# Two 64-column stationary tiles in place of one of 128, in the level products of a delta scan

## What is computed

```python
kk = jnp.einsum('bhntd,bhnsd->bhnts', k, k)
M = jnp.eye(CHUNK, dtype=jnp.float32) + jnp.where(strict, kk * decay * beta[..., :, None], 0.0)
...
U = lax.linalg.triangular_solve(M, v * beta[..., None], left_side=True, lower=True, unit_diagonal=True)
Wk = lax.linalg.triangular_solve(M, k * (beta * eG)[..., None], left_side=True, lower=True, unit_diagonal=True)
```

## Time and profile before

| | us |
|---|---|
| median of 3 runs | 3254.94 |
| lowest and highest run | 3253.11, 3256.28 |
| span of the profiled execution | 3254.3 |
| PE busy in that span | 3039.7 (93%) |
| weight loads busy (PEld) | 2229.6 (69%) |
| DVE busy | 963.2 (30%) |
| ACT busy | 577.3 (18%) |
| stretch of the delta scan in that span | 1946 to 2352 |

### The profile page before, as it was taken

One profiled execution on the slowest core, in us unless ns is written; L12 is line 12 of the kernel. 1 busy time (PEld: TensorE's weight loads), 2 busy tenths in 40 slices (PEclk: granted clock), 3 DMA queues, 4 the chain that ended last, 5 costly groups with the idle time before them and its releaser, 6 DMA issues.

```text
span 3254.3 us, 43264 instructions
## 1 busy us (share of the span) xinstructions
PE 3039.7 (93%) x18405; PEld 2229.6 (69%) x18405; DVE 963.2 (30%) x2408; ACT 577.3 (18%) x1297; POOL 96.0 (3%) x145
## 2 busy tenths in 40 slices
PE   6999999797999999997999989999986999999994
PEld 1465479745887777771456459999944888777773
DVE  1100136643001000102177536666645010001002
ACT  3100111240000000003167212222242000000002
POOL 0000000000000000000000000000000000000000
PEclk9899998897999999998999999999997999999997
DMA  8411100217999999957411100000016899999992
GB/s 281 154 52 52 45 1 1 65 62 270 312 311 303 303 309 308 306 183 271 155 52 52 39 0 1 1 2 1 1 65 224 279 314 304 307 305 307 306 310 87
DMA packets 276365, 545.50 MB, mean 168 GB/s; under 512 B 15233, under 2 KB 23817, under 8 KB 276233
## 3 DMA queue, kind: packets, MB, share of 16 engines
q1 hardware_dynamic: 175049, 328.64, 29.4%
q10 hardware_dynamic: 93600, 188.75, 16.6%
q0 software_dynamic: 7584, 26.22, 3.2%
HBM read 517.89 MB, written 25.70 MB: 167 GB/s over the span
## 4 chain that ended last, share of the span: by engine, by line
PE 88%; DVE 6%; ACT 3%; DMA 2%; issue 1%; SPq 0%; DVEq 0%; POOL 0%; ACTq 0%
PE ps L1204 28%; PE ps L1215 14%; PE ps L803 8%; PE ps L813 6%; PE ps L760 5%; PE ps L1139 3%; PE ps L1101 3%; PE ps L804 2%; PE ps L1083 2%; PE ps L880 1%; PE ps L1115 1%; PE ps L791 1%; PE ps L950 1%; PE ps L966 1%; ACT L424 1%; ACT L423 1%
## 5 line engine op out<-in xcount | busy, mean ns | idle before, releaser
L1204 PEld LDWEIGHTS ps<-wk,slots 128*128 128x128 f32 x6144 | 691.1, 192 | 16.5 <-issue 16.0
L1204 PE MATMUL ps<-wk,slots 128*128 128x80 f32 x6144 | 689.9, 275 | 0.0
L1215 PE MATMUL ps<-qkv,og 128*80 128x512 f32 x1024 | 446.7, 594 | 2.4 <-DVE og L1748 1.3
L1215 PEld LDWEIGHTS ps<-qkv,og 128*80 128x80 f32 x1024 | 151.0, 150 | 275.5 <-issue 268.0
L803 PE MATMUL ps<-hT,slots 128*128 128x512 f32 x640 | 334.0, 604 | 3.1 <-ACT hT L455 3.1
L1204 PE MATMUL ps<-wk,qkv 128*128 128x80 f32 x2048 | 233.9, 275 | 0.0
L1204 PEld LDWEIGHTS ps<-wk,qkv 128*128 128x128 f32 x2048 | 231.3, 192 | 0.0
L804 PEld LDWEIGHTS ps<-hT,slots 128*128 128x128 f32 x640 | 123.5, 193 | 156.6 <-issue 156.6
L813 PE MATMUL ps<-slots,hT 128*128 128x512 f32 x480 | 209.3, 596 | 0.0
L760 PE MATMUL ps<-slots,cnd 128*2 128x512 f32 x384 | 172.0, 602 | 35.1 <-DVE x L1776 24.1
L1724 DVE COPY idc<-idT 80x1 uint32 (+1 forms) x32 | 4.8, 149 | 612.8 <-DMA moe_d<-og,idc 612.7
(11 more groups left out here) (261 smaller groups left out, 3228.5 us busy)
## 6 DMA issues: line engine op xcount, KB each, us to landing
slots<-in_w_gate_dram ACTq DMA_DIRECT2D x60, 2048.0 KB, 9.2
qkv<-in_w_down_dram SPq DMA_DIRECT2D x34, 2048.0 KB, 9.8
slots<-in_w_up_dram SPq DMA_DIRECT2D x32, 2048.0 KB, 10.2
qkv<-in_w_up_dram SPq DMA_DIRECT2D x32, 2048.0 KB, 7.8
qkv<-in_w_down_dram ACTq DMA_DIRECT2D x30, 2048.0 KB, 7.8
slots<-in_w_ada_dram SPq DMA_DIRECT2D x24, 2048.0 KB, 8.1
slots<-in_w_in_dram SPq DMA_DIRECT2D x16, 2048.0 KB, 8.1
slots<-in_w_out_dram SPq DMA_DIRECT2D x4, 2048.0 KB, 16.2
```

The lines of the kernel that those rows point to most:

```text
L1204: ins = mm(PS[:, j, fb * CAP:(fb + 1) * CAP], slot[j][:, kt, fb * P:(fb + 1) * P], xsT[q][:, kt, :], start=(kt == 0), stop=(kt == KT - 1))
L1215: ins = mm(PS[0:CAP, 4 + j, :], hdT[:, ft, :], slot[4 + j][:, ft, :], start=(ft == 0), stop=(ft == KT - 1))
```

## The change

Both level products of levels 1 to 5 are split by the columns of the stationary operand. A loop over `s` takes columns 0 to 63 and then 64 to 127, as a matmul of its own each, with the same moving operand of 64 columns, and the result goes to PSUM partitions 0 to 63 and 64 to 127. So each of the 800 matmuls becomes two; waits and increments stay where they were, the increment on the last matmul of the four heads. Nothing changes on the other engines, nor in the order of the work.

```diff
--- before.py
+++ after.py
@@ -1080,8 +1080,10 @@
                                 pe.wait_ge(S("dl_cm"), at_mid(u, l, p))
                                 pe.wait_ge(S("dl_d"), at_early(u, l - 1, p))
                                 for h in range(4):
-                                    ins = mm(pack(four(PS[:, bx, :])[:, :, 0:64], l)[:, h], B["CM"][l % 2][:, h, :],
-                                             cols1(B["D"][:, h, :], l, d), start=True, stop=True)
+                                    for s in range(2):
+                                        ss_ = slice(64 * s, 64 * s + 64)
+                                        ins = mm(pack(four(PS[ss_, bx, :])[:, :, 0:64], l)[:, h], B["CM"][l % 2][:, h, ss_],
+                                                 cols1(B["D"][:, h, :], l, d), start=True, stop=True)
                             else:
                                 pe.wait_ge(S("dl_d"), at_early(u, l - 1, p))
                                 for h in range(4):
@@ -1098,7 +1100,10 @@
                             pe.wait_ge(S("dl_dt"), at_all(u, l - 1, p))
                             for h in range(4):
                                 if l < LEVELS - 1:
-                                    ins = mm(hb(2 * p + l % 2, h, 64), B["DT"][:, h, :], B["X"][:, h, :], start=True, stop=True)
+                                    for s in range(2):
+                                        ss_ = slice(64 * s, 64 * s + 64)
+                                        ins = mm(PS[ss_, 2 * p + l % 2, h * P:h * P + 64], B["DT"][:, h, ss_], B["X"][:, h, :],
+                                                 start=True, stop=True)
                                 else:
                                     ins = mm(PS[first, 2 * p, h * P:h * P + 64], B["X"][then, h, :],
                                              B["DT"][then, h, then], start=True, stop=True)
```

## The result

The changed kernel takes 3224.22 us (median of 4 runs, 3219.37 to 3228.59), the kernel before 3254.03 (4 runs): the ratio is 0.9906, with a 95% interval of 0.9892 to 0.9920. It is 30 us faster. The forecast was 3275; the rival with overlapping halves said 3220. The profiled execution's own time is 3221.31, its span 3219.5, against 3254.3 before: -34.8 us. Runs of the kernel before in the experiments' sessions had medians of 3253.2 to 3256.9, so each run is given with its ratio to the kernel before in its own session; "better than the changed kernel" is a difference of medians.

A forecast was written before the change was run, and what follows sets the result against it. TensorE was taken to bound the delta scan. Serial halves 0.16 plus switches 0.14 and 0.15 gave 0.45 us a level, 22.5 us over 5 levels and 10 units, less 2.2 hidden: +20.3, 3275 us, range 3216 to 3284.

The forecast's parts named there:

- the rival with overlapping halves: In the scan's level products both column halves work at the same time, 58 ns a pair: 3220 us; chance 0.36.
- What bounds the kernel: In the delta scan TensorE, busy 401.25 of 406.00 us, leads except where VectorE holds the chain.
- The load sets the pace: At L1083 the 128-column loads start 111 ns apart; streaming 64 columns lies inside the load.
- The price of two halves: In the level products a pair costs 58 to 116 ns; 116 taken against 111 before, +0.16 us a level.
- the serial case: The forecast's own case: halves in the level products run one after the other, 3275 us, 3262 to 3284; chance 0.48.
- The switch of tile size: Going into the level products' smaller tiles costs 0.14 us a level, going back out 0.15.
- The serial sum: Over the scan, 0.45 us a level makes 22.5 us, less 2.2 hidden at level 1: +20.3 us.
- limit of 95 ns a pair: In the level products, overlap makes the kernel faster once a pair of halves costs under about 95 ns.

The follow-up runs named there:

- the serial run: Changed kernel with both matmuls of each pair sent through the same column half, the other half of both products left unwritten; 3274.9 us, ratio to before 1.0056.

## Why the prediction was wrong

**What bounds the kernel: right.** TensorE led the scan, and what it gained came out at the end.

**The load sets the pace: right.** Every product with a 128-column load that was split gained: with 64 streaming columns, with 80, and with one. With 80 a pair costs 69 ns and not 58, so there the load alone is no longer the pace.

**The price of two halves: wrong, and this is the step that failed.** I wrote that the price of a pair lies between 58 and 116 ns and took 116, "because the row it is nearest to is the only one with 64-column tiles, and because the order is unkind". The run with both matmuls in one half has 116 and 3274.9 us; the changed kernel has 58 and 3224. The row I leaned on could not decide: all its passes used one place of the array, so it was a row on serial work, and nearness in shape is not nearness in the question asked. The second reason was wrong as well: the halves apart by eight passes still overlapped in part, so two passes of one half in a row do not hold up the other.

The trace after agrees with the sentence of the Trainium skill that the forecast had set aside ("TensorEngine Tiling (Array Packing)", section Tiling Modes: different tiles can execute LdWeights and Matmul in parallel): 59 ns for a pair, loads included. With two claims and no row on either, 0.48 to 0.36 for the serial case had nothing in the trace to rest on.

**The switch of tile size: right.** 0.14 in: the loader is idle 0.17 us at 40 entries. 0.15 out: eight passes of L880 take 1.09 us behind L1105, and 0.95 behind L1101 at the same level in the kernel before; 0.14 more:

```profile
2132.78 0.95 PE ps L880 x8
```

**The serial sum: right in size.** +20 us forecast; the serial run's ratio of 1.0056 is +18.

**The overlap rival's working: right in its sum, with errors that cancel.** It had -0.64 for a level with a mask product, the switches included. The chain after has 0.64 + 0.02 + 0.42 + 0.60 + 0.35 + 0.04 + 0.69 = 2.76, the way in included, and 0.14 for the way out: 2.90 against 3.52, -0.62. The parts are not those of the working: VectorE starts 0.66 us into the level, not 0.47 + 0.14 + 0.23 = 0.84, and the last product takes 0.69, not 0.47. Level 5: 0.64 + 0.02 + 0.43 + 0.04 + 1.15 + 0.14 = 2.42, -1.10, against -1.11. At level 1 it was too hopeful: -0.48 by the working, while eight of the ten units gain 0.27 to 0.29 there, by the starts of their passes. It said 3220 for 3224. Its limit of 95 ns a pair does not follow from its own rows: 0.29 us of switches over 32 passes is 9 ns, so 102; nothing rests on it.

**The range** from 3216 to 3284 held the time because it was drawn round both cases, not because the forecast's mechanism came true: the kernel got faster where slower was forecast. The case that happened was in the text with its mechanism and its price; the choice between the two was the mistake.

## What to carry to other kernels

Where the loads of a TensorE group start at the same distance whatever streams (here 111 to 112 ns with 1, 64 and 80 columns), the load is the pace, and two matmuls on the two column halves, standing next to each other, cut it to 59 ns with 64 columns and to 69 with 80, at about 0.3 us for each excursion to the smaller tile. Do it stage by stage, and look afterwards for who leads: in the scan it was VectorE's order of work, in the expert stage still TensorE, with pauses that go with the fetching of twice as many instructions. When the nearest row shows the right shape doing another thing, give the other end of the range the same chance, or ask the chip with a run that changes only that.

## What was not expected of the hardware

- The granted clock in the mLSTM scan went from 0.88 to 0.99 when 16 load-bound one-column passes were put into half the time. In the nine profiles of this case without that edit it is 0.88 to 0.90 from 450 to 585 us. Idleness does not go with the lower level here: in the changed kernel TensorE counts as busy for 10.00 of 10.00 us from 513 to 523 at the full clock, and it is at 0.50 from 525 to 527.
- The DMA share of 0.92 at 308 GB/s looked like a limit next to a TensorE that is always busy. It went to 0.98 and 337 GB/s once TensorE was faster, and even there the weights landed 12 us or more ahead of their use.
- Pauses of up to 3.0 us, 162 us in all, came into the expert stages with the longer program, each ending 1.2 to 1.7 us after a packet of instructions had landed. The profile's waits call them "issue" and name no engine.
- TensorE reaches about three passes ahead for the other half of the array, as the run with the halves apart shows.
